# Differential attention: the squares of heads 0 to 6 computed on GpSimd, with two halving additions before VectorE's sum

## Chip, cores and metric

One Trainium2 chip, one of its cores. The metric is device microseconds from the first to the last instruction of the program. The kernel before takes 2082.36 us, the median of three runs (2082.19 to 2086.64).

## What is computed

The program runs two transformer stacks one after the other, each of two layers, over 256 tokens of width 1024. The first has gated feed-forward blocks, a short convolution and a sparse attention; the second has a differential attention and a grouped-query attention, each followed by a feed-forward block. The change lies in the differential attention alone. Of the reference, that part is:

```python
def attend(qb, keys, vals):
    s = jnp.einsum('bhmtd,bhmsd->bhmts', pair(qb), keys).astype(f32) * DIFF_DH ** -0.5
    p = jax.nn.softmax(s, axis=-1)
    a = (p[:, :, 0] - lam * p[:, :, 1]).astype(vals.dtype)
    return jnp.einsum('bhts,bhse->bhte', a, vals)

def finish(o):
    o = rmsnorm(o, subln) * (1.0 - lambda_init)
    return o.transpose(0, 2, 1, 3).reshape(Bt, Lt, DIFF_HEADS * 2 * DIFF_DH) @ w_out
```

There are 8 heads with outputs of 128 columns, and 512 queries: 256 latent tokens, which see 512 keys, and 256 context tokens, which see 256 keys. The `rmsnorm` in `finish` needs the sum of the squares of each head's 128 output columns, for every query. That sum is what the change computes in another way.

## The kernel before

The whole program is one `trace` function that writes five instruction streams by hand, one for each engine, with semaphore waits between them; no scheduler sets the order. Blocks are called sub-blocks s0 to s10, and the differential attention is s7. Queries lie in 4 tiles of 128 rows (the partitions), so that a head is 4 jobs: jobs 4h and 4h+1 are latent tiles with 512 keys ("full"), jobs 4h+2 and 4h+3 are context tiles with 256 keys ("half"). There are 32 jobs, J = 0 to 31.

Each job goes through these steps, and every engine has its own loop over J:

- TensorE computes the two score maps of the job into two PSUM banks (L2566), later transposes the combined probabilities (L2656), and later still multiplies them by the values (L2670). Its order for an index J is: scores of J, transposes of J-3, value product of J-4. The scores of J wait for the exponentials of J-2, since two bank pairs alternate; the transposes of J-3 wait for VectorE's step `p` of that job; the value product waits for ScalarE's copy of the transposes.
- VectorE takes the negated row maximum (L1898, `neg`), and for the job before, J-1, the reciprocal of a denominator (L1906), the coefficient (L1908, `coef`, 128x1, two inputs in SBUF) and the combination of the two maps (L1910, `p`, 128x512 or 128x256, two inputs in SBUF).
- ScalarE copies the transposes of J-3 out of PSUM (L1295, `evT`), then computes the two exponentials of J (L1270, `exp`).

When a head's four value products are done, ScalarE at index J = 4h+7 copies its output (128x512) from PSUM to SBUF (L1308, `evO`, the tile `ada`) and squares it into `silu_t[:, h % 2, :]` (L1312, `osq`). VectorE sums each group of 128 squares into one number, 4 per partition (L1890, `osum`), at its index J = 4h+8, behind step `p` of job 4h+7.

After the loop comes the tail. VectorE adds the epsilon term to the sums of heads 0 to 6 (L1920, `omean`), ScalarE takes the root (L1288, `root`, at its index 33, ahead of its copies of job 31 and of head 7's output), VectorE takes the reciprocal (L1925) and scales the heads (L1938, `on`); head 7 goes the same way a little later. TensorE transposes the scaled heads (L2685), ScalarE copies them (L1320), and the product with the output weights begins (L2305).

GpSimd does nothing in this sub-block. Its work elsewhere in the program is the low part of activations (L845, L853) and, in the sparse attention, a multiplication (L861).

Of the kernel before, what the change touches and what calls it, by code (L numbers as in the profile page):

```python
# [8 lines left out]
ALU = mybir.AluOpType  # L9
# [53 lines left out]
def trace(nc, t, io, out, stop):  # L63
    ctx = ExitStack()
    with ctx:
# [735 lines left out]
        def _(pool):  # L801
# [53 lines left out]
            def nsa_pool(tag):  # L855

                for J, (g_, tt, br, nk) in enumerate(nsa_jobs):
# [3 lines left out]
                    t.done(g.tensor_tensor(pr, pr, cf, ALU.mult), pool_s, (tag, "scaled", J))  # L861

            for s in subs:
                if s["T"] == 256:
                    for tt in range(2):
                        for k0, n in () if dve_lo(s) and tt else groups(s, tt):
                            lo(s, k0, n, tt)
                else:
                    for c in s["cs"][0:1] if second_pairs(s) and not pairs_late(s) else s["cs"]:
                        for k in s["ks"]:  # L870
                            lo_pair(s, k, c)
                if s["kind"] == "nsa":
                    nsa_pool(f"s{s['n']}")


        @block.scalar
        def _(act):
# [405 lines left out]
            def diff_act(s, tag, w):  # L1283
# [6 lines left out]
                for J in range(len(jobs) + 4):  # L1290
# [13 lines left out]
                    if 0 <= J - 4 and jobs[J - 4][1] == 3:  # L1304

                        h = jobs[J - 4][0]
                        act.wait_ge(pe_s, t.at((tag, "pv", J - 4)))
                        t.done(a.copy(w.qT[:, h, :], bank[6 + h % 2][:, :]), act_s, (tag, "evO", h))  # L1308
                        act.wait_ge(act_s, t.at((tag, "evO", h)))
                        if h >= 2:  # L1310
                            act.wait_ge(dve_s, t.at((tag, "osum", h - 2)))
                        t.done(a.activation(silu_t[:, h % 2, :], w.qT[:, h, :], ACT.Square), act_s, (tag, "osq", h))  # L1312
# [102 lines left out]
        def _(dve):  # L1415
# [470 lines left out]
            def diff_dve(s, tag, w):  # L1886
                jobs = diff_jobs
                def osum(h):
                    dve.wait_ge(act_s, t.at((tag, "osq", h)))
                    t.done(v.reduce_sum(ada_row[:, 4 * h:4 * h + 4], silu_t[:, h % 2, :].rearrange("p (t d) -> p t d", t=4), AX_X), dve_s, (tag, "osum", h))  # L1890
                for J in range(len(jobs) + 1):
# [9 lines left out]
                    if 0 <= J - 1:  # L1901
# [8 lines left out]
                        t.done(v.scalar_tensor_tensor(out=p0, in0=p1, scalar=d_coef(i), in1=p0, op0=ALU.mult, op1=ALU.add), dve_s, (tag, "p", i))  # L1910
                    if J >= 8 and J % 4 == 0:
                        osum((J - 8) // 4)
                gate(s, tag, 1)

                def means(a0, a1):
# [940 lines left out]
```

## Time and profile before

| | |
|---|---|
| median of three runs | 2082.36 us (2082.19 to 2086.64) |
| span of the profiled execution | 2082.3 us; the page gives no other time for it |
| TensorE, share of the span busy | 97% |
| VectorE | 66% |
| ScalarE | 45% |
| GpSimd | 4%, 121 instructions |
| mean granted TensorE clock | 0.991 |
| attention jobs of s7 in the trace | from about 1261.7 us to 1340 us |

The profiled execution's span agrees with the median to 0.1 us, so differences can be made against either. The shares are averages over eleven sub-blocks with different limits; for the change the stretch of s7 counts, and there each engine's own rows have to be read in order of time. VectorE's and ScalarE's durations are those of each instruction; consecutive instructions overlap by about 0.08 us, so the distance between two starts is shorter than the duration. Ends of TensorE's matmuls are modelled.

### The profile page before, as it was taken

The numbers are of one execution on the slowest core, as the hardware profiler recorded it, in microseconds if no ns is written. First come the engines' busy times: TensorE is split into PE (matmuls) and PEld (weight loads), VectorE is DVE, ScalarE is ACT, GpSimd is POOL, SyncE is SP. The second block draws the span as 40 slices with busy tenths as digits, with TensorE's granted clock in tenths as the row PEclk, the third lists the DMA queues.
The fourth block names the chain that finished last, engine by engine and source line by source line (L and its number), as shares of the span: only waits on it lengthen the run. The fifth ranks groups of instructions, "written<-read, shape, count | busy, mean of one in ns | idle before, by whom it ended". The sixth has DMA issues, their size and how long they took to land.

```text
span 2082.3 us, 32485 instructions
## 1 busy us (share of the span) xinstructions
PE 2024.0 (97%) x12969; PEld 1766.2 (85%) x12969; DVE 1377.4 (66%) x1936; ACT 940.4 (45%) x1420; POOL 88.9 (4%) x121
## 2 busy tenths in 40 slices
PE   6999999999999999999999999999999999999999
PEld 4998898998899987569988886688888888878997
DVE  3768798768976776657766756866555335855454
ACT  4344535334643445663355446842222323655342
POOL 1000000000100000310001000010000001100000
PEclk8999999999999999999999999999999999999999
DMA  9897877888877885647954321035344231425553
GB/s 348 277 316 281 297 260 263 302 271 313 273 257 268 303 292 188 226 148 264 303 180 152 113 90 41 12 111 174 130 139 164 81 112 61 142 81 198 180 177 113
DMA packets 240469, 411.32 MB, mean 198 GB/s; under 512 B 10236, under 2 KB 179669, under 8 KB 240341
## 3 DMA queue, kind: packets, MB, share of 16 engines
q1 hardware_dynamic: 239744, 409.31, 57.2%
q8 instruction: 89, 1.46, 0.3%
q14 instruction: 39, 0.32, 0.0%
q10 hardware_dynamic: 597, 0.23, 0.0%
HBM read 408.47 MB, written 1.05 MB: 197 GB/s over the span
## 4 chain that ended last, share of the span: by engine, by line
PE 79%; DVE 12%; ACT 4%; DMA 2%; issue 2%; SPq 0%; POOL 0%; DVEq 0%; ACTq 0%
PE bank L2305 21%; PE bank L2202 14%; PE bank L2204 13%; PE bank L2203 13%; DVE w_lo L1424 3%; PE bank L2395 2%; PE bank L2397 2%; PE bank L2396 2%; DVE gate_b L1480 2%; DMA xs<-in_ada_w 1%; DVE mid L1586 1%; PE bank L2154 1%; PE bank L2566 1%; ACT w_hi L890 1%; DVE astat L1898 1%
## 5 line engine op out<-in xcount | busy, mean ns | idle before, releaser
L1424 DVE TENSOR_TENSOR w_lo<-stage,w_hi 128x2048 fp32r<-128x2048 f32 x255 | 582.1, 2290 | 405.4 <-ACT w_hi L890 405.3
L890 ACT CAST w_hi<-stage 128x2048 fp32r<-128x2048 f32 x255 | 485.7, 1906 | 639.9 <-PE bank L2305 208.9
L2202 PE MATMUL bank<-h_hi,w_hi 128*128 128x256 f32 (+1 forms) x2336 | 699.3, 299 | 0.8 <-DVE w_lo L1424 0.8
L2203 PE MATMUL bank<-h_lo,w_hi 128*128 128x256 f32 (+1 forms) x2336 | 696.3, 298 | 0.0
L2204 PE MATMUL bank<-h_hi,w_lo 128*128 128x256 f32 (+1 forms) x2336 | 696.3, 298 | 0.0
L2202 PEld LDWEIGHTS bank<-h_hi,w_hi 128*128 128x128 f32 x2336 | 447.8, 192 | 14.3 <-DVE w_lo L1424 1.1
L2204 PEld LDWEIGHTS bank<-h_hi,w_lo 128*128 128x128 f32 x2336 | 447.7, 192 | 12.5
L2203 PEld LDWEIGHTS bank<-h_lo,w_hi 128*128 128x128 f32 x2336 | 447.8, 192 | 12.3
L2305 PE MATMUL bank<-w_hi,h_hi 128*128 128x512 f32 x776 | 244.0, 392 | 2.1 <-DVE mid L2066 1.2
L2305 PE MATMUL bank<-w_lo,h_hi 128*128 128x512 f32 x776 | 242.6, 390 | 0.0
L2305 PE MATMUL bank<-w_hi,h_lo 128*128 128x512 f32 x776 | 242.5, 390 | 0.0
L1480 DVE SCALAR_TENSOR_TENSOR gate_b<-ada,cond,gate_b 128x1024 f32<-128x1024 f32 x182 | 231.7, 1283 | 6.6 <-DMA ada<-in_kv_ada_w 1.2
L2305 PEld LDWEIGHTS bank<-w_hi,h_hi 128*128 128x128 f32 x776 | 144.3, 188 | 32.6 <-issue 1.7
L2305 PEld LDWEIGHTS bank<-w_hi,h_lo 128*128 128x128 f32 x776 | 145.8, 188 | 30.4
L2305 PEld LDWEIGHTS bank<-w_lo,h_hi 128*128 128x128 f32 x776 | 145.8, 188 | 30.4
L1367 ACT ACTIVATE silu_t<-bank 128x256 f32<-128x256 f32 (+1 forms) x132 | 53.7, 417 | 202.7 <-PE bank L2204 192.4
L1997 DVE TENSOR_TENSOR mid<-silu_t,bank 128x256 f32 (+3 forms) x132 | 60.1, 462 | 94.6 <-PE bank L2204 93.4
L1433 DVE TENSOR_TENSOR h_lo<-mid,h_hi 128x512 fp32r<-128x512 f32 (+1 forms) x82 | 64.3, 785 | 23.2 <-ACT h_hi L921 23.2
L2395 PE MATMUL bank<-w_hi,h_hi 128*128 128x512 f32 x192 | 75.9, 395 | 0.4 <-DVE w_lo L1424 0.4
L2397 PE MATMUL bank<-w_hi,h_lo 128*128 128x512 f32 x192 | 74.9, 390 | 0.0
L2396 PE MATMUL bank<-w_lo,h_hi 128*128 128x512 f32 x192 | 74.8, 390 | 0.0
L853 POOL TENSOR_TENSOR h_lo<-mid,h_hi 128x256 fp32r<-128x256 f32 x40 | 31.8, 822 | 831.4 <-ACT h_hi L994 831.4
(275 smaller groups left out, 2100.5 us busy)
## 6 DMA issues: line engine op xcount, KB each, us to landing
ada<-in_ada_w SPq DMA_DIRECT2D x114, 1024.0 KB, 5.5
stage<-in_ffn_w_in SPq DMA_DIRECT2D x88, 1024.0 KB, 9.1
stage<-in_ffn_w_out SPq DMA_DIRECT2D x44, 1024.0 KB, 5.1
stage<-in_ffn_w_gu SPq DMA_DIRECT2D x44, 1024.0 KB, 5.2
stage<-in_ffn_w_down SPq DMA_DIRECT2D x22, 1024.0 KB, 4.9
stage<-in_a_w_in SPq DMA_DIRECT2D x12, 1024.0 KB, 7.5
stage<-in_diff_w_in SPq DMA_DIRECT2D x12, 1024.0 KB, 5.4
ada<-in_kv_ada_w SPq DMA_DIRECT2D x8, 1024.0 KB, 7.4
```

What stands on the lines that cost most here:

```text
L890: a.copy(w_hi[:, s, :], stage[:, s, :]).then_inc(hi_done, 1)
L1424: v.tensor_tensor(w_lo[:, s, :], stage[:, s, :], w_hi[:, s, :].bitcast(F32), ALU.subtract).then_inc(lo_done, 1)
L1433: v.tensor_tensor(h_lo[:, r], mid[:, bass.ds(c, 2 * T)], h_hi[:, r].bitcast(F32), ALU.subtract).then_inc(mlo_done, 1)
L1480: ins = v.scalar_tensor_tensor(out=acc[c], in0=w, scalar=cond[:, b, kk, c:c + 1], in1=acc[c], op0=ALU.mult, op1=ALU.add)
L1997: v.tensor_tensor(mid[:, bass.ds(o, T)], silu_t[:, q, 0:T], bank[up_bank(s, j, i) + 2 + q][:, 0:T], ALU.mult).then_inc(mid_done, 1)
L2202: m.matmul(dst[:, 0:T], wh, h_hi[:, h0:h0 + T], start=(k == ks[0]), stop=False)
L2203: m.matmul(dst[:, 0:T], wh, h_lo[:, h0:h0 + T], start=False, stop=False)
L2204: ins = m.matmul(dst[:, 0:T], wl, h_hi[:, h0:h0 + T], start=False, stop=(k == ks[-1]))
L2305: ins = m.matmul(y_bank(T, tt, h)[:, :], a_[:, r:r + P], w_[:, slot, kc * D + h * 512:kc * D + (h + 1) * 512], start=first and n == 0, sto ...
L2395: m.matmul(bank[tt][:, :], h_hi[:, r], w_hi[:, slot, c], start=(k == 4), stop=False)
L2396: m.matmul(bank[tt][:, :], h_hi[:, r], w_lo[:, slot, c], start=False, stop=False)
L2397: ins = m.matmul(bank[tt][:, :], h_lo[:, r], w_hi[:, slot, c], start=False, stop=(k == 1))
```

## The change

For heads 0 to 6 ScalarE no longer squares. GpSimd waits for ScalarE's copy of the head, multiplies the head by itself (128x512), adds the upper 64 columns of each group of 128 to the lower 64 (4x64 numbers per partition), and the upper 32 of those to the lower 32 (4x32). Each of the three instructions waits for the one before it. VectorE then sums 32 numbers per group instead of 128. Head 7 is squared and summed as before. VectorE's sum of head h moves from index J = 4h+8 to J = 4h+10; the sum of head 6 then has no index in the loop and stands behind it.

```diff
+            def diff_pool(tag, w):
+
+                for J in range(len(diff_jobs) + 2):
+                    if J >= 9 and J % 4 == 1:
+                        h = (J - 9) // 4
+                        sq = silu_t[:, h % 2, :]
+                        pool.wait_ge(act_s, t.at((tag, "evO", h)))
+                        if h >= 2:
+                            pool.wait_ge(dve_s, t.at((tag, "osum", h - 2)))
+                        t.done(g.tensor_tensor(sq, w.qT[:, h, :], w.qT[:, h, :], ALU.mult), pool_s, (tag, "osq512", h))
+                        sq = sq.rearrange("p (t d) -> p t d", t=4)
+                        for n in (64, 32):
+                            pool.wait_ge(pool_s, t.at((tag, f"osq{8 * n}", h)))
+                            t.done(g.tensor_tensor(sq[:, :, 0:n], sq[:, :, 0:n], sq[:, :, n:2 * n], ALU.add), pool_s, (tag, "osq" if n == 32 else "osq256", h))
+
...
@@ -1306,9 +1323,10 @@
                         h = jobs[J - 4][0]
                         act.wait_ge(pe_s, t.at((tag, "pv", J - 4)))
                         t.done(a.copy(w.qT[:, h, :], bank[6 + h % 2][:, :]), act_s, (tag, "evO", h))
+                        if h < 7:
+                            continue
                         act.wait_ge(act_s, t.at((tag, "evO", h)))
-                        if h >= 2:
-                            act.wait_ge(dve_s, t.at((tag, "osum", h - 2)))
+                        act.wait_ge(dve_s, t.at((tag, "osum", h - 2)))
                         t.done(a.activation(silu_t[:, h % 2, :], w.qT[:, h, :], ACT.Square), act_s, (tag, "osq", h))
...
                 def osum(h):
-                    dve.wait_ge(act_s, t.at((tag, "osq", h)))
-                    t.done(v.reduce_sum(ada_row[:, 4 * h:4 * h + 4], silu_t[:, h % 2, :].rearrange("p (t d) -> p t d", t=4), AX_X), dve_s, (tag, "osum", h))
+                    n = P if h == 7 else P // 4
+                    dve.wait_ge(act_s if h == 7 else pool_s, t.at((tag, "osq", h)))
+                    t.done(v.reduce_sum(ada_row[:, 4 * h:4 * h + 4], silu_t[:, h % 2, :].rearrange("p (t d) -> p t d", t=4)[:, :, 0:n], AX_X), dve_s, (tag, "osum", h))
...
-                    if J >= 8 and J % 4 == 0:
-                        osum((J - 8) // 4)
+                    if J >= 10 and J % 4 == 2:
+                        osum((J - 10) // 4)
                 gate(s, tag, 1)
+                osum(6)
```

On VectorE, around head 0's sum, the order before is this. `gate_b` and `mid` hold the probabilities, `astat` the maxima and coefficients, `silu_t` the squares.

```order
L1910 SCALAR_TENSOR_TENSOR mid<-mid,astat 128x256
L1890 TENSOR_REDUCE ada_row<-silu_t 128x4
L1898 TENSOR_REDUCE astat<-bank 128x2
L1906 RECIPROCAL astat<-ada_row 128x1
L1908 SCALAR_TENSOR_TENSOR astat<-astat,stat,ada_row 128x1
L1910 SCALAR_TENSOR_TENSOR gate_b<-gate_b,astat 128x512
```

The same place of the changed kernel, where VectorE's lines are higher by 19:

```order
L1929 SCALAR_TENSOR_TENSOR mid<-mid,astat 128x256
L1917 TENSOR_REDUCE astat<-bank 128x2
L1925 RECIPROCAL astat<-ada_row 128x1
L1927 SCALAR_TENSOR_TENSOR astat<-astat,stat,ada_row 128x1
L1929 SCALAR_TENSOR_TENSOR gate_b<-gate_b,astat 128x512
L1917 TENSOR_REDUCE astat<-bank 128x2
L1925 RECIPROCAL astat<-ada_row 128x1
L1927 SCALAR_TENSOR_TENSOR astat<-astat,stat,ada_row 128x1
L1929 SCALAR_TENSOR_TENSOR gate_b<-gate_b,astat 128x512
L1909 TENSOR_REDUCE ada_row<-silu_t 128x4
L1917 TENSOR_REDUCE astat<-bank 128x2
```

The sum has moved behind two more jobs' steps, from in front of the maximum of a full job to in front of the maximum of a half job.

On GpSimd, which had nothing between the low parts of s7 and those of s8, this stands now for each of the heads 0 to 6:

```order
L853 TENSOR_TENSOR h_lo<-mid,h_hi 128x256 x16
L872 TENSOR_TENSOR silu_t<-ada 128x512
L876 TENSOR_TENSOR silu_t<-silu_t 128x4x64
L876 TENSOR_TENSOR silu_t<-silu_t 128x4x32
L872 TENSOR_TENSOR silu_t<-ada 128x512
```

In the tail, VectorE's last two jobs and head 6's sum stand in this order in the changed kernel; head 6's sum has kept its place:

```order
L1929 SCALAR_TENSOR_TENSOR mid<-mid,astat 128x256
L1925 RECIPROCAL astat<-ada_row 128x1
L1927 SCALAR_TENSOR_TENSOR astat<-astat,stat,ada_row 128x1
L1929 SCALAR_TENSOR_TENSOR mid<-mid,astat 128x256
L1909 TENSOR_REDUCE ada_row<-silu_t 128x4
L1937 TENSOR_TENSOR ada_row<-ada_row 128x28
L1940 SCALAR_TENSOR_TENSOR ada_row<-ada_row 128x28
```

## Rows read from the trace of the kernel before

**Rows 1.** Window of 10 us: busy us of PE, PEld, DVE, ACT, POOL; clock; DMA.

```profile
1295.00:1305.00 10.00, 9.75 (x64) 6.50 (x66) 9.51 (x23) 9.31 (x28) 0.00 (x0) 1.00 0.00 0
```

**Rows 2.** Chain of waits: start us, us, what. Part of one head.

```profile
1299.38 1.23 DVE astat L1898
...
1301.36 0.68 DVE ada_row L1890
```

**Rows 3.** Timeline of TensorE: start us, us. Scores of jobs 4, 8, 12.

```profile
1273.71 1.13 PE L2566 MATMUL bank<-mid,ada 64*128 64x512 f32 x4 [0.83 <-ACT mid L1270]
...
1281.85 1.13 PE L2566 MATMUL bank<-mid,ada 64*128 64x512 f32 x4
...
1290.02 1.13 PE L2566 MATMUL bank<-mid,ada 64*128 64x512 f32 x4
```

**Rows 4.** Timeline of VectorE, jobs 10 to 12 of the loop.

```profile
1298.79 0.48 DVE L1910 SCALAR_TENSOR_TENSOR mid<-mid,astat 128x256 f32<-128x256 f32 x1
1299.38 1.23 DVE L1898 TENSOR_REDUCE astat<-bank 128x2 f32<-128x1024 f32 x1
...
1300.70 0.22 DVE L1908 SCALAR_TENSOR_TENSOR astat<-astat,stat,ada_row 128x1 f32<-128x1 f32 x1
1300.96 0.48 DVE L1910 SCALAR_TENSOR_TENSOR mid<-mid,astat 128x256 f32<-128x256 f32 x1
1301.36 0.68 DVE L1890 TENSOR_REDUCE ada_row<-silu_t 128x4 f32<-128x512 f32 x1
1301.96 1.21 DVE L1898 TENSOR_REDUCE astat<-bank 128x2 f32<-128x1024 f32 x1
```

**Rows 5.** Timeline of ScalarE, the same stretch; idle time before it in brackets.

```profile
1299.37 0.58 ACT L1308 COPY ada<-bank 128x512 f32<-128x512 f32 x1
...
1303.21 0.69 ACT L1270 ACTIVATE gate_b<-bank,astat 128x512 f32<-128x512 f32 x1 [0.51 <-DVE astat L1898]
```

**Rows 6.** Groups by line of GpSimd, shapes apart: count | busy us, mean ns.

```profile
L845 POOL TENSOR_TENSOR h_lo<-mid,h_hi 128x512 fp32r<-128x512 f32 x14 | 18.8, 1359 | 863.4 <-ACT h_hi L978 863.4
L861 POOL TENSOR_TENSOR gate_b<-gate_b,w 128x512 f32<-128x512 f32 x8 | 8.3, 1040 | 44.4 <-DVE w L1794 44.4
...
L845 POOL TENSOR_TENSOR h_lo<-mid,h_hi 128x256 fp32r<-128x256 f32 x6 | 4.3, 740 | 0.4 <-ACT h_hi L978 0.4
...
L845 POOL TENSOR_TENSOR h_lo<-mid,h_hi 128x128 fp32r<-128x128 f32 x4 | 1.8, 461 | 19.1 <-ACT h_hi L978 19.1
```

**Rows 7.** Timeline of VectorE and GpSimd, sparse attention.

```profile
827.37 1.04 POOL L861 TENSOR_TENSOR gate_b<-gate_b,w 128x512 f32<-128x512 f32 x1 [37.49 <-DVE w L1794]
...
827.70 0.79 DVE L1773 TENSOR_TENSOR mid<-mid,w 128x60 f32<-128x60 f32 x1
...
842.10 0.22 DVE L1773 TENSOR_TENSOR mid<-mid,w 128x60 f32<-128x60 f32 x1
```

**Rows 8.** Timeline of VectorE and GpSimd, grouped-query attention.

```profile
1778.15 2.29 DVE L1424 TENSOR_TENSOR w_lo<-stage,w_hi 128x2048 fp32r<-128x2048 f32 x1
1779.14 3.27 POOL L853 TENSOR_TENSOR h_lo<-mid,h_hi 128x256 fp32r<-128x256 f32 x3 [13.89 <-ACT h_hi L994]
```

**Rows 9.** Timeline of GpSimd, start of the program: the second waits for the first.

```profile
5.30 0.40 POOL L825 CAST mid<-mid 128x256 f32<-128x256 int32 x1
5.84 0.40 POOL L827 TENSOR_SCALAR_AFFINE_SELECT mid<-mid 128x256 f32<-128x256 f32 x1
```

**Rows 10.** Timeline of VectorE, a sum over 128 numbers per partition.

```profile
1141.86 0.29 DVE L1816 TENSOR_REDUCE stat<-mid 128x2 f32<-128x128 f32 x1
```

**Rows 11.** Timelines of ScalarE and VectorE in the tail, in order of time.

```profile
1332.06 0.58 ACT L1308 COPY ada<-bank 128x512 f32<-128x512 f32 x1
...
1332.72 0.48 DVE L1910 SCALAR_TENSOR_TENSOR mid<-mid,astat 128x256 f32<-128x256 f32 x1
...
1334.23 0.19 DVE L1920 SCALAR_TENSOR_TENSOR ada_row<-ada_row 128x28 f32<-128x28 f32 x1
...
1335.45 0.23 ACT L1288 ACTIVATE ada_row<-ada_row 128x28 f32<-128x28 f32 x1
```

More of the change, by code:

```diff
@@ L873, in _ @@
                     nsa_pool(f"s{s['n']}")
+                elif s["kind"] == "diff":
+                    diff_pool(f"s{s['n']}", Wide(s))
         @block.scalar
```

## The prediction

> **What bounds the kernel now.** I read first the busy time of the stretch in which the change lies. Inside the loop over jobs TensorE is busy for 9.75 us of 10, VectorE for 9.51, ScalarE for 9.31 and GpSimd for none [rows 1]. Three engines are nearly full, so shares don't say which one sets the pace. The chain of waits is next: in each head it passes through VectorE's maximum and through its sum of squares [rows 2], 0.68 us that stand once in every head. By the chain alone one would expect a gain from a shorter sum. The timeline of TensorE answers that expectation. The scores of jobs 4, 8 and 12 start at 1273.71, 1281.85 and 1290.02 us [rows 3]. The distances are 8.14 and 8.17 us. The first distance holds no sum and no square at all, since head 0's output is copied only after it, and the second holds one of each. A whole square with a whole sum thus cost 0.03 us per head. TensorE's own work, and the order in which it takes the jobs, sets a period of about 8.14 us, and VectorE follows it with little to spare: its step `p` of job 10 starts at 1298.79, takes 0.48, of which about 0.08 overlap what follows, and the next maximum starts at 1299.38 [rows 4]. That is 0.19 us of idle time per head. ScalarE has 0.51 us of idle time in front of one exponential, where it waits for VectorE's maximum [rows 5].
>
> **The change, part by part, in one head.**
>
> ScalarE loses a square of 0.63 us. It was idle for 0.51 us of each head already and waits for VectorE there [rows 5], so I cost this gain at nothing in the loop. What hides it is ScalarE's wait for the maximum.
>
> VectorE loses a sum of 0.68 us, 0.60 from start to start (1301.36 to 1301.96) [rows 4]. It gains one over 4x32 numbers two jobs later. A sum over 128 numbers took 0.29 us [rows 10], so 0.21 after the same overlap. The relief is 0.39 us per head. It can be cashed only down to TensorE's 8.14, so at most 0.03 per head.
>
> GpSimd gets three instructions. The nearest rows for the square are 1.36 us (a subtraction, 128x512) and 1.04 us (a multiplication of the same size in which one operand repeats); the additions are 0.74 and 0.46 us by their sizes [rows 6]. I take 1.31 for the square, near the upper row, since both of its operands run through all numbers, and 0.72 and 0.44 for the additions, a little under the means, which contain disturbed cases. The Trainium skill's page "GPSIMD Engine Reference", section Performance versus the Vector engine, gives 4497 ns for an addition of 2048 numbers; a quarter of it, an estimate of 1.12 us, would make the square's hold below shorter by 0.2 us in each head. The three take 2.47 us and two hand-overs. A hand-over from one GpSimd instruction to the next that waits for it was 0.14 us (5.30 + 0.40 to 5.84) [rows 9]. From the end of ScalarE's copy, 1299.95 [rows 5], the squares are ready at about 1302.8. The short sum stands two jobs behind the old place at 1301.36 [rows 4], and a job is a quarter of 8.17 us, so it is due at about 1305.4; nobody waits for GpSimd in the loop. It was idle there, so its own work is free.
>
> What isn't free is the memory access. Two rows of the sparse attention show it: VectorE's L1773, 128x60 with two inputs in SBUF, takes 0.22 us, but 0.79 when it starts at 827.70, inside a GpSimd multiplication that ends at 828.41, and it ends 0.08 us after that end [rows 7]. The other way round, three GpSimd instructions of 0.74 [rows 6] took 3.27 us, 1.05 too many, where the first began 1.3 us before the end of a VectorE instruction with two SBUF inputs (1778.15 + 2.29) [rows 8]. The later one stands still until the earlier one is through. The Trainium skill's page "SBUF — State Buffer", section Who interferes with whom, states the rule, which speaks against this change: a VectorE instruction with two SBUF inputs and a GpSimd instruction that reads SBUF exclude each other for the whole of whichever came first, while a `tensor_reduce` is never held. The trace agrees for the two pairs shown. Had the two engines been free of each other, the sum would be that of the third rival below.
>
> Now the place. The copy of a head ends at 1299.95, so the square runs from about 1300.03 to 1301.34. `coef` of job 11, two SBUF inputs, is due at 1300.70 [rows 4]. It ends about 1301.42 instead of 1300.92: 0.50 us late (0.25 with the lower price of the square). Then `p` of job 11 and GpSimd's first addition are both due within 0.1 us of each other. `p` needs `coef`'s end and about 0.04 (1300.92 to 1300.96 [rows 4]), so it is due at 1301.46; the addition is due at 1301.34 and a hand-over of 0.14, at 1301.48. I take it that `p` wins. Then the addition waits, is over about 1302.5, and the second one about 1303.1, beside a maximum that reads PSUM and isn't held. VectorE's account for the head is 0.50 - 0.60 + 0.21 = +0.11 us, less than its 0.19 of slack. Against that the delay comes in one lump, between a maximum and the transposes that wait for `p`, so I don't cost it at nothing: 0.10 us per head, with 0 and 0.2 as ends. For the six heads inside the loop this is **+0.6 us**.
>
> **The tail.** Head 6's copy ends at 1332.64 [rows 11]. GpSimd starts at about 1332.72, in the same moment as the last `p` [rows 11]; without a hold it is done after 2.47 and two hand-overs of 0.14, at 1335.5. The short sum, 0.29, ends at 1335.85 and the epsilon step, 0.19 [rows 11], at 1336.1. ScalarE's root, which waited for its table and started at 1335.45 [rows 11], starts then. That is 0.65 later. Behind the root on ScalarE's queue stand the copy of job 31's transposes, the gate's copies, head 7's copy and its square, and TensorE's last value product waits for the first of these; I take it that nothing in that queue has time to spare. ScalarE's missing square doesn't help, as it would only wait longer at the root. So the tail costs **+0.6 us**, with +0.1 (square of 1.04, short hand-overs) and +1.2 (the square held by the last `p`) as ends.
>
> After s7 the down product follows on TensorE, which is the bound again, and hands the delay on. Nothing moves on SP's queue; no DMA is touched.
>
> The sum is 0.6 + 0.6 = 1.2 us on 2082.3, and the median is the same to 0.1: **2083.6 us**. A measurement of this kernel can tell about 0.2%, 4.2 us, from no change.
>
> **The rivals.**
>
> The first ends slower. GpSimd's addition gets in front of `p` in each head. It decides by 0.02 us in my account above: with a hand-over under 0.12 us, the addition goes first. Then the addition runs from 1301.44 to 1302.16, and `p` of job 11 ends at about 1302.50 (the last 0.34 of its 0.48 are left, by the overlap that L1773 showed) instead of 1301.94: another 0.56 us. The account is 1.06 - 0.60 + 0.21 = +0.67; less the 0.19 of slack, and with the same 0.10 for the lump, it is 0.58 per head, 3.5 for six, and with 0.7 for the tail 2086.5. With the square at 1.04 it is 2084.9; if the last addition also catches a `coef`, 0.44 less slack, near 2088.5. For it: the order is nearly a tie, and VectorE's 9.51 of 10. Against it: the measured 0.14.
>
> The second is that the relief counts in full. VectorE is on the chain of waits [rows 2], and 0.39 us in seven heads is 2.7 us: 2079.6. Against it stands the first head with no sum and the same period [rows 3].
>
> The third is that the change does nothing that can be seen: `coef` is so small that it isn't held, or GpSimd's square falls beside the maximum only. Then the loop gains 0.03 x 6 = 0.2 and the tail takes 0.2 to 0.6: 2082.5.
>
> **How the numbers follow.** My forecast has 0.44, the slow rival 0.27, the neutral one 0.21, the gain 0.08. Of the slow rival a little over half lies above 2086.5, which makes 0.15 for slower by over 0.2%. A gain of over 4.2 us would need more than the whole relief, so I leave 0.03, for what I haven't seen. The rest, 0.82, is within 0.2%. The range leaves out the gain below and the upper part of the slow rival: 2081.6 to 2087.2.
>
> **What would show it.** In the profile after, the distance of every fourth score should be 8.2 to 8.3 us from head 2 on; about 8.7 would be the slow rival, 8.14 the neutral one. L1927 should have a longest instance near 0.7 us in each head, beside many of 0.22, and L1929 should stay at 0.75 and 0.48; a L1929 above 1 us in each head is the slow rival. GpSimd's addition of 4x64 should be longer than 0.74 where `p` holds it. The root should start about 1.2 us later. I am wrong if GpSimd's square takes over 1.6 us, if the summed squares come so late that VectorE waits for them, or if the period falls under 8.1.

## The result, and the profile after

The changed kernel takes 2093.96 us, the median of five runs (2089.05 to 2096.19). The kernel before takes 2085.93 (2082.19 to 2087.99), the median of five too, of which three are the runs that I started from. The ratio is 1.0036, with an interval of 1.0026 to 1.0047: 7.5 us slower by the ratio, 8.0 between the medians, and outside my range of 2081.6 to 2087.2. The profiled execution of the changed kernel took 2089.05 us, with a span of 2087.3 at a mean granted clock of 0.990.

Lines from 1890 on are higher by 19 or 20 now: the maximum is L1917, `coef` L1927, `p` L1929, VectorE's sum L1909. GpSimd's square is L872, its additions L876. The same window as [rows 1], and the next one; the columns are those of [rows 1]:

```profile
1295.00:1305.00 10.00, 9.56 (x65) 6.35 (x63) 9.65 (x21) 8.63 (x26) 3.38 (x5) 1.00 0.01 2
1305.00:1315.00 10.00, 9.56 (x66) 6.42 (x62) 9.72 (x19) 8.19 (x25) 3.47 (x5) 1.00 0.00 0
```

VectorE lost 0.40 us of work per head and is yet busier than before (9.65 and 9.72 against 9.51), while TensorE is down from 9.75 to 9.56. Something has made VectorE's instructions longer. The timeline of VectorE in the same place as [rows 4], the last half job of head 2 and what follows, shows which:

```profile
1302.98 1.22 DVE L1917 TENSOR_REDUCE astat<-bank 128x2 f32<-128x1024 f32 x1
1304.12 0.15 DVE L1925 RECIPROCAL astat<-ada_row 128x1 f32<-128x1 f32 x1
1304.31 0.57 DVE L1927 SCALAR_TENSOR_TENSOR astat<-astat,stat,ada_row 128x1 f32<-128x1 f32 x1
1304.92 1.03 DVE L1929 SCALAR_TENSOR_TENSOR mid<-mid,astat 128x256 f32<-128x256 f32 x1
1305.88 1.21 DVE L1917 TENSOR_REDUCE astat<-bank 128x2 f32<-128x1024 f32 x1
```

And the timeline of GpSimd beside it:

```profile
1303.83 1.04 POOL L872 TENSOR_TENSOR silu_t<-ada 128x512 f32<-128x512 f32 x1 [6.05 <-ACT ada L1325]
1304.95 1.32 POOL L876 TENSOR_TENSOR silu_t<-silu_t 128x256 f32<-128x256 f32 x2
```

`coef` takes 0.57 instead of 0.22. It is held until about the end of the square: 1303.83 + 1.04 = 1304.87, and `coef` ends at 1304.88. Then `p` takes 1.03 instead of 0.48. The first addition runs inside it, from 1304.95 for about 0.74 us, and `p` ends at 1305.95, some 0.26 us behind that addition's end. The addition itself is not lengthened. So in heads 1 to 5 both instructions are held, 0.35 and 0.55 us, and it is `p` that stands still, not the addition. In head 0 `coef` is held for 0.15 only (it takes 0.37), which is why the second distance below is shorter than the later ones; in head 6 `p` alone is held, for 0.84. The groups of GpSimd, shapes apart, show the durations over all seven heads:

```profile
L872 POOL TENSOR_TENSOR silu_t<-ada 128x512 f32<-128x512 f32 x7 | 7.3, 1039 | 175.5 <-ACT ada L1325 175.5
L876 POOL TENSOR_TENSOR silu_t<-silu_t 128x256 f32<-128x256 f32 x7 | 5.2, 736 | 0.5
L876 POOL TENSOR_TENSOR silu_t<-silu_t 128x128 f32<-128x128 f32 x7 | 3.5, 507 | 0.5
```

The square costs 1.04 us, the lower of my two prices. TensorE now waits, here as in the heads around it, for an exponential that waited for VectorE's late maximum. The first row is TensorE's, the scores of a half job; the second ScalarE's, the exponential before it:

```profile
1308.63 0.70 PE L2586 MATMUL bank<-mid,ada 64*128 64x256 f32 x4 [0.44 <-ACT gate_b L1287]
```

```profile
1307.12 0.69 ACT L1287 ACTIVATE gate_b<-bank,astat 128x512 f32<-128x512 f32 x1 [0.87 <-DVE astat L1917]
```

ScalarE's wait was 0.51 us there before [rows 5].

**A local measure.** All executions of this program spread over some 10 us, so I read each profile in the stretch that the change can touch: from the scores of job 4 (the first of [rows 3]) to the start of the product with the output weights (the expectations below call it the down product), and in it the distances of every fourth score. Read from TensorE's timeline of each profile, in us:

| kernel | scores of job 4 start | distances of jobs 4, 8, ... 28 | stretch |
|---|---|---|---|
| before | 1273.71 | 8.14 8.17 8.18 8.17 8.18 8.17 | 70.31 |
| after | 1276.88 | 8.14 8.30 8.49 8.48 8.49 8.49 | 72.44 |
| e1_same_before | 1277.67 | 8.14 8.18 8.18 8.17 8.17 8.18 | 70.32 |
| e2_same_after | 1281.23 | 8.14 8.29 8.50 8.48 8.49 8.49 | 72.43 |
| e3_add_after_p | 1279.37 | 8.15 8.14 8.15 8.14 8.14 8.15 | 70.86 |
| e4_no_sums | 1279.42 | 8.14 8.14 8.15 8.15 8.14 8.15 | 70.14 |
| e5_square_only | 1275.90 | 8.14 8.14 8.33 8.34 8.33 8.33 | 71.06 |
| e6_writes_only | 1275.79 | 8.14 8.14 8.15 8.14 8.14 8.14 | 69.78 |
| e7_square_after_p | 1275.19 | 8.14 8.15 8.27 8.43 8.43 8.42 | 72.81 |
| e8_same_after | 1282.40 | 8.15 8.29 8.48 8.48 8.49 8.48 | 72.41 |
| e9_extra_sum | 1275.05 | 8.14 8.76 8.76 8.76 8.76 8.77 | 73.84 |
| e10_three_heads | 1280.40 | 8.15 8.29 8.48 8.49 8.15 8.16 | 71.61 |
| e11_same_after | 1272.13 | 8.14 8.30 8.49 8.48 8.49 8.50 | 72.43 |
| e12_wider_add | 1278.78 | 8.13 8.58 8.75 8.76 8.75 8.76 | 74.33 |

The same kernel repeats its stretch within 0.03 us, where the whole time varies by several us. Two single executions, of 3116.69 us in e1 and of 5746.66 us in e2, lie far outside this spread and are left out of all ratios. In the stretch the change costs 2.1 us: 1.9 up to the start of the last `p` (59.01 us from the scores of job 4 before, 60.90 after) and 0.2 behind it. The measured 7.5 us are more than that; what lies in the rest is taken up with e8 and e11.

### The profile page after: what moved, and what is told of

Same layout as the page of the kernel before. It is cut to its first block, busy times and chain, and to the rows that moved or that the text cites. A ratio compares the mean times of both kernels' runs of the same rounds, so it can differ in the third digit from the quotient of the medians.

```text
span 2087.3 us, 32499 instructions
## 1 busy us (share of the span) xinstructions
PE 2026.0 (97%) x12969; PEld 1767.2 (85%) x12969; DVE 1380.2 (66%) x1936; ACT 937.6 (45%) x1413; POOL 104.9 (5%) x142
## 4 chain that ended last, share of the span: by engine, by line
PE 81%; DVE 10%; ACT 4%; issue 2%; DMA 2%; SPq 0%; POOL 0%; DVEq 0%; ACTq 0%
PE bank L2325 20%; PE bank L2222 14%; PE bank L2224 14%; PE bank L2223 14%; DVE w_lo L1442 2%; PE bank L2415 2%; PE bank L2417 2%; PE bank L2416 2%; DVE gate_b L1498 1%; PE bank L2586 1%; DVE mid L1604 1%; DMA xs<-in_ada_w 1%; PE bank L2174 1%; ACT w_hi L907 1%; PE bank L2564 1%
## 5 line engine op out<-in xcount | busy, mean ns | idle before, releaser
L845 POOL TENSOR_TENSOR h_lo<-mid,h_hi 128x512 fp32r<-128x512 f32 (+2 forms) x24 | 24.9, 1059 | 882.1 <-ACT h_hi L995 882.1
```

## The experiments

The kernels were timed in three batches: e1 to e4, e5 to e8, e9 to e12. The kernels of one batch share the runs of the kernel before; each has 12 runs of its own. Ratios are to the kernel before of the same batch. Diffs are against the changed kernel where nothing else is said.

### e1_same_before and e2_same_after: how well the two kernels repeat

Both kernels again, unchanged.

> The kernel before, unchanged, measured against itself. It shows how far two sets of runs of one kernel lie apart, and with which granted clocks. Between the profiles of before and after, job 4's scores start 3.2 us later (1273.71 against 1276.88), ahead of anything the change touches; from there to the first down product it is 70.3 us before and 72.4 after, so only 2.1 us belong to the changed stretch. Theory A (the change costs about 2 us, the rest of the 8 us between the medians is the clock's chance): this kernel's own runs spread by 5 to 8 us too, with clocks between 0.986 and 0.991, and the time follows the clock. Theory B (the change costs 7 to 8 us by itself, by some effect outside its stretch): this kernel's runs stay near 2082 to 2086 with a clock near 0.991, and only the changed kernel goes to 2090 and more.

> The changed kernel, unchanged, once more. Theory A: the ratio to the kernel before is 1.001, within 0.2% of 1, when clocks are alike, and the stretch from job 4's scores to the down product is again 72.4 us in the profile. Theory B: the ratio is again 1.003 to 1.004 and the clock is again lower than that of the kernel before.

The kernel before gave 0.9995 [0.9982, 1.0008], the changed one 1.0018 [1.0006, 1.0030]. The stretches came out at 70.32 and 72.43, as in the first profiles. The sign is sure; the size of the first comparison, 1.0036, is not repeated.

### e3_add_after_p: the first addition waits for `p`

```diff
                             pool.wait_ge(pool_s, t.at((tag, f"osq{8 * n}", h)))
+                            if n == 64:
+                                pool.wait_ge(dve_s, t.at((tag, "p", 4 * h + 7)))
```

> One wait more: GpSimd's first addition of head h also waits for VectorE's step p of job 4h+7, so that the addition can't get in front of it. The slow rival says that the addition's hold of p (1.04 us where 0.48 is normal) makes the period 8.49 us instead of 8.17. If so, p takes 0.48 again in this kernel, only coef stays held (0.57), the period of every fourth score goes back to 8.14 to 8.2, and the stretch from job 4's scores to the down product is 70.3 to 71 us. If instead the held coef or GpSimd's square makes the period, it stays near 8.4 to 8.5 and the stretch above 72.

The ratio is 0.9997 [0.9984, 1.0009], and the stretch is 70.86 instead of 72.44. The timeline of VectorE, the same place (its lines are higher by two, and the whole is 2.0 us later):

```profile
1306.31 0.57 DVE L1929 SCALAR_TENSOR_TENSOR astat<-astat,stat,ada_row 128x1 f32<-128x1 f32 x1
1306.92 0.48 DVE L1931 SCALAR_TENSOR_TENSOR mid<-mid,astat 128x256 f32<-128x256 f32 x1
1307.52 1.23 DVE L1919 TENSOR_REDUCE astat<-bank 128x2 f32<-128x1024 f32 x1
```

and of GpSimd:

```profile
1305.83 1.04 POOL L872 TENSOR_TENSOR silu_t<-ada 128x512 f32<-128x512 f32 x1 [5.17 <-ACT ada L1327]
1307.55 1.26 POOL L878 TENSOR_TENSOR silu_t<-silu_t 128x256 f32<-128x256 f32 x2 [0.68 <-DVE mid L1931]
```

`coef` is still held by 0.35 (0.16 in head 0), `p` is back at 0.48, and every distance is back at 8.14 to 8.15. So the hold of `p` is what the loop pays for, and the hold of `coef` alone fits under TensorE's period. This is the order that my forecast assumed. With it the loop is even 0.03 us per head faster than before; the 0.10 us per head that I had put on the lump of delay does not exist. What is left, +0.55 us, is all in the tail.

### e4_no_sums: the relief by itself, at its largest

Against the kernel before: ScalarE doesn't square heads 0 to 5, VectorE doesn't sum them, and their sums are the constant 1.

```diff
                         t.done(a.copy(w.qT[:, h, :], bank[6 + h % 2][:, :]), act_s, (tag, "evO", h))
+                        if h < 6:
+                            continue
...
-                    if J >= 8 and J % 4 == 0:
-                        osum((J - 8) // 4)
+                    if J == 32:
+                        osum(6)
```

> From the kernel before: heads 0 to 5 are neither squared nor summed on any engine (their sums are the constant 1), heads 6 and 7 as before. If TensorE's work sets the period, it is 8.14 us instead of 8.17 and the stretch from job 4's scores to the down product falls by 0.2 us from 70.3. If VectorE's sum on the chain of waits is worth its time, the stretch falls by 6 x 0.60 = 3.6 us and the period to about 7.6.

The ratio is 0.9999 [0.9986, 1.0012]; the stretch is 70.14, so six squares and six sums, 7.9 us of work on two engines, are worth 0.17 us in all. The distances are TensorE's 8.14. The time went into waiting. VectorE's timeline has this in front of the maximum of job 4h+8:

```profile
1307.57 1.23 DVE L1899 TENSOR_REDUCE astat<-bank 128x2 f32<-128x1024 f32 x1 [0.47 <-PE bank L2567]
```

The `p` before it starts at 1306.62 and takes 0.48, and the next instruction can follow 0.08 before an end, so 1307.57 - 1307.02 = 0.55 us are free in this place. VectorE's sum of 0.60 used to fill them and stood out by 0.05, which is the 0.03 that the distances show.

### e5_square_only: the square on GpSimd, no additions

GpSimd squares, and VectorE sums all 128 numbers per group, two jobs later as in the changed kernel.

```diff
-                        t.done(g.tensor_tensor(sq, w.qT[:, h, :], w.qT[:, h, :], ALU.mult), pool_s, (tag, "osq512", h))
...
+                        t.done(g.tensor_tensor(sq, w.qT[:, h, :], w.qT[:, h, :], ALU.mult), pool_s, (tag, "osq", h))
...
-                    n = P if h == 7 else P // 4
+                    n = P
```

> From the changed kernel: GpSimd's two additions are gone, VectorE sums all 128 numbers of each group at the new place. With no addition nothing can hold p, but coef is still held by the square (0.57 instead of 0.22). Theory (VectorE's account against TensorE's period, holds counted): per head +0.35 for coef, the sum costs 0.60 as before, slack 0.19, so the period is 8.3 to 8.45 us and p takes 0.48 everywhere but at head 6. If only the hold of p matters and a late coef is free, the period is 8.14 to 8.18, since VectorE's work is then that of the kernel before.

The ratio is 1.0002 [0.9988, 1.0016], with a stretch of 71.06. `coef` is held (0.58), `p` is not, except in the last head. The distances of 8.33 are 0.19 above TensorE's, although only 0.36 are held: here the whole sum of 0.60 stands two jobs later. What is free behind that place are the 0.19 us in front of the next head's maximum of 4h+7 and what the hold leaves of the 0.55 in front of that of 4h+8, 0.19 too. That leaves 0.22 over.

### e6_writes_only: GpSimd as busy, but reading nothing

The square and the additions are replaced by writes of the constant 1, so the sums are those of ones.

```diff
-                        t.done(g.tensor_tensor(sq, w.qT[:, h, :], w.qT[:, h, :], ALU.mult), pool_s, (tag, "osq512", h))
+                        t.done(g.memset(sq, 1.0), pool_s, (tag, "osq512", h))
...
-                            t.done(g.tensor_tensor(sq[:, :, 0:n], sq[:, :, 0:n], sq[:, :, n:2 * n], ALU.add), pool_s, (tag, "osq" if n == 32 else "osq256", h))
+                            t.done(g.memset(silu_t[:, h % 2, :], 1.0), pool_s, (tag, "osq" if n == 32 else "osq256", h))
```

> From the changed kernel: each of GpSimd's three instructions is a memset of 128x512 numbers in silu_t, about 0.5 us each, at the same place and with the same waits. GpSimd is then busy for about 1.5 us beside coef and p, but reads nothing. If the hold is one of reading (two inputs of VectorE against GpSimd's reads), coef takes 0.22 and p 0.48 throughout, and the period is 8.14 us. If any GpSimd instruction holds VectorE's, coef or p is longer in every head and the period is above 8.2.

The ratio is 0.9991 [0.9976, 1.0006], with a stretch of 69.78. The groups of VectorE, shapes apart:

```profile
L1929 DVE SCALAR_TENSOR_TENSOR mid<-mid,astat 128x256 f32<-128x256 f32 x14 | 6.8, 484 | 0.5
L1927 DVE SCALAR_TENSOR_TENSOR astat<-astat,stat,ada_row 128x1 f32<-128x1 f32 x28 | 6.1, 220 | 1.0
```

Nothing is held, though each of GpSimd's three writes takes 0.52 us, they begin in the same place, and in each of heads 1 to 5 the second begins inside `coef` and lasts into `p`. So writing SBUF doesn't hold VectorE; what the held cases have beside it is GpSimd's reading. The Trainium skill's page "SBUF — State Buffer", section Who interferes with whom, names the same pair, a VectorE instruction with two SBUF inputs and a GpSimd instruction that reads SBUF, "not with one that only writes it"; the trace agrees on both halves, with 0.57 against 0.22.

### e7_square_after_p: the square itself waits for `p`

```diff
+                        pool.wait_ge(dve_s, t.at((tag, "p", 4 * h + 7)))
                         t.done(g.tensor_tensor(sq, w.qT[:, h, :], w.qT[:, h, :], ALU.mult), pool_s, (tag, "osq512", h))
```

> From the changed kernel: GpSimd's square of head h waits for VectorE's step p of job 4h+7, so that all three of GpSimd's instructions come later by one step. The same work, the same order on VectorE. If the place of GpSimd's instructions against VectorE's decides, the first addition now meets coef of the full job 4h+8 and the second meets its p, and the period is 8.3 to 8.5 us although job 4h+7 is never held. If a late start frees VectorE, as the wait in the third experiment did (8.15), the period is 8.14 to 8.2.

The ratio is 1.0011 [0.9997, 1.0025], with a stretch of 72.81: locally no better than the change. VectorE's timeline, one job further on:

```profile
1304.80 0.60 DVE L1928 SCALAR_TENSOR_TENSOR astat<-astat,stat,ada_row 128x1 f32<-128x1 f32 x1
1305.43 1.04 DVE L1930 SCALAR_TENSOR_TENSOR gate_b<-gate_b,astat 128x512 f32<-128x512 f32 x1
```

and of GpSimd:

```profile
1303.54 1.04 POOL L873 TENSOR_TENSOR silu_t<-ada 128x512 f32<-128x512 f32 x1 [6.05 <-DVE mid L1930]
1304.66 1.26 POOL L877 TENSOR_TENSOR silu_t<-silu_t 128x256 f32<-128x256 f32 x2
```

The square now lies beside the maximum, which it doesn't hold, but the two additions behind it outlast the maximum. From head 2 on they catch `coef` and the longer `p` of the next job, 0.38 and 0.29 us. Waiting for the right instruction is not enough: what is released by it must also be through before VectorE's next pair of reads. e3 has only the additions there, and they are, by 0.04 us: in the place shown above the second ends at 1308.81, and the next `coef` starts at 1308.85.

### e8_same_after and e11_same_after: the changed kernel again

Unchanged, beside the kernels of the second and of the third batch.

> The changed kernel once more, on the chip and in the hour of the three above, for the ratio alone: 1.0036 and 1.0018 were measured so far, 1.0010 is what its own stretch (72.4 against 70.3 us) accounts for. If the remainder is chance of the clock, this ratio may fall anywhere from 0.999 to 1.003; if it belongs to the kernel, it is again 1.0015 or more.

> The changed kernel a fourth time, beside the two above, for the ratio: 1.0036, 1.0018 and 1.0022 so far. If the excess over the 1.0010 of its own stretch is the kernel's, it is again above 1.0015; if it was chance, between 0.9995 and 1.0025.

The ratios are 1.0022 [1.0008, 1.0035] and 1.0017 [1.0004, 1.0030], with stretches of 72.41 and 72.43. These and e2 ask what lies outside the stretch. The changed kernel reached the scores of job 4 at 1276.88, 1281.23, 1282.40 and 1272.13 us in its four profiles, the kernel before at 1273.71 and 1277.67. The code up to there is the same in both, and the earliest of all is a run of the changed kernel. So no profile shows a delay that belongs to the change and lies ahead of it. None shows one behind the stretch either: from the start of the product with the output weights to the end it takes 737.97, 738.24, 737.90 and 740.31 us in the changed kernel's four profiles, 738.27 and 738.02 in those of the kernel before. The 740.31 are e11's, whose clock was 0.97 from 1800 to 1850 us, where that of the kernel before was 1.00. What moves ahead of the stretch is the granted clock. Windows of the stretch with the sparse attention, for the kernel before, for the changed kernel, and for e11:

```profile
750.00:1000.00 250.00, 240.36 (x1657) 189.56 (x1656) 170.50 (x449) 132.11 (x295) 31.01 (x28) 0.97 0.65 222
```

```profile
750.00:1000.00 250.00, 239.43 (x1627) 188.12 (x1626) 168.35 (x447) 128.77 (x291) 31.00 (x28) 0.95 0.63 216
```

```profile
750.00:1000.00 250.00, 240.38 (x1664) 189.73 (x1663) 170.38 (x448) 131.72 (x293) 31.03 (x28) 0.97 0.65 222
```

The changed kernel of the first profile ran at 0.95 there, e11 at 0.97 like the kernel before. Over the 252 executions with a listed clock (without the two left out above), a fit with one offset per kernel and one slope gives 1.5 us more for each 0.001 of mean clock less, and the single executions lie between about 0.984 and 0.992. The 40 of the changed kernel have a mean of 2092.3 us at 0.9878, 116 of the kernel before 2087.4 at 0.9888. Of these 4.9 us the stretch has 2.1, the clock about 1.4, and 1.4 (with an uncertainty of about 0.7) I can't place. My expectations don't decide whether this is chance: the repetitions came out at 1.0017 to 1.0022, above the 1.0015 that I had set for an excess of the kernel's own, but in e8 and e11 also inside the range that I had given to chance. The stretch alone accounts for 1.0010. Why the mean clock of the changed kernel's runs was lower, in each of the three batches, stays open too.

### e9_extra_sum: VectorE made later in the same place, without GpSimd

Against the kernel before, an extra sum over 96 numbers per group in front of the real one, heads 0 to 5.

```diff
                     dve.wait_ge(act_s, t.at((tag, "osq", h)))
+                    if h < 6:
+                        t.done(v.reduce_sum(ada_row[:, 4 * h:4 * h + 4], silu_t[:, h % 2, :].rearrange("p (t d) -> p t d", t=4)[:, :, 0:96], AX_X), dve_s, (tag, "extra", h))
+                        dve.wait_ge(dve_s, t.at((tag, "extra", h)))
```

> From the kernel before: for heads 0 to 5 VectorE sums 4x96 of the squares once more in front of each head's sum, about 0.5 us from start to start, and GpSimd does nothing. It slows VectorE as much as the holds do, by other means. Theory (a period of 8.14 by TensorE and 0.19 us of slack on VectorE): the period is 8.4 to 8.55 us and the stretch from job 4's scores to the down product 71.8 to 72.5. As to the 3 us by which the changed kernel's runs lie above its own stretch: if they come with any slower loop, this kernel's runs also lie some 4 to 5 us above the kernel before; if they need GpSimd, only by about 2 us.

The ratio is 1.0017 [1.0004, 1.0030], with a stretch of 73.84, 3.5 us more. I had expected at most 72.5, and a distance of at most 8.55. VectorE's timeline:

```profile
1303.47 0.49 DVE L1913 SCALAR_TENSOR_TENSOR mid<-mid,astat 128x256 f32<-128x256 f32 x1
1303.88 0.55 DVE L1891 TENSOR_REDUCE ada_row<-silu_t 128x4 f32<-128x384 f32 x1
1304.46 0.69 DVE L1893 TENSOR_REDUCE ada_row<-silu_t 128x4 f32<-128x512 f32 x1
```

The extra sum delays the maximum by 0.58 us and the distance grows by 0.59, from 8.17 to 8.76. In front of this maximum the kernel before had nothing left to absorb. The 0.19 us of idle time that I had counted as slack stand elsewhere, in front of the maximum before it (1299.38 in [rows 4]), and are still there in e9. The delay needs no GpSimd: time that VectorE loses here is lost whatever takes it. The measured time agrees with the stretch, 3.5 us by both. It shows no excess like the changed kernel's, though its interval, 0.8 to 6.3 us, is too wide to exclude one of 1.4.

### e10_three_heads: half a dose

GpSimd squares heads 0 to 2 alone; ScalarE squares the others and VectorE sums them whole, at the new place.

```diff
-                    if J >= 9 and J % 4 == 1:
+                    if J >= 9 and J % 4 == 1 and J < 21:
...
-                        if h < 7:
+                        if h < 3:
```

> From the changed kernel: only heads 0 to 2 go through GpSimd, heads 3 to 7 are squared by ScalarE and summed by VectorE in full, at the new places. The period should be 8.3 to 8.5 where heads 1 and 2 are held and 8.17 from then on, and the tail as in the kernel before, since GpSimd isn't in it: the stretch is 70.31 plus about 0.6 = 70.9 to 71.1 us. If the additions' hold isn't what costs, the period stays 8.4 or more to the end.

The ratio is 1.0011 [0.9998, 1.0024], with a stretch of 71.61, where I had expected at most 71.1. Three distances are those of the changed kernel (8.29, 8.48, 8.49), and with the next one the loop is back at 8.15, with a whole sum two jobs later. The holds leave no trace behind them; each head pays for itself. The stretch is 1.3 us longer, of which the distances have 0.71. The other 0.59 lie behind job 28, where nothing of GpSimd runs: from the scores of job 28 to the last `p` it takes 10.59 us (1330.12 to 1340.71) against 10.00 before. That is the size of head 5's whole sum, 0.60. My reading, which no run tests by itself, is that at the new place it has no later head whose free time takes it up, so the moved sum is paid for once, at the end.

### e12_wider_add: the first addition made longer

The first addition takes 96 numbers per group instead of 64, so the sums are others.

```diff
-                            t.done(g.tensor_tensor(sq[:, :, 0:n], sq[:, :, 0:n], sq[:, :, n:2 * n], ALU.add), pool_s, (tag, "osq" if n == 32 else "osq256", h))
+                            m_ = 96 if n == 64 else 32
+                            t.done(g.tensor_tensor(sq[:, :, 0:m_], sq[:, :, 0:m_], sq[:, :, P - m_:P], ALU.add), pool_s, (tag, "osq" if n == 32 else "osq256", h))
```

> From the changed kernel: GpSimd's first addition is over 4x96 numbers instead of 4x64 (the sums are then others). By GpSimd's own rows (0.74 us for 256, 0.46 for 128) it takes 1.02 instead of 0.74. If p stands still for the whole addition, p of job 4h+7 takes 1.3 us instead of 1.04 and the period is 8.49 + 0.28 = 8.77 us, the stretch 74 us or a little more. If the hold is a fixed price per meeting, p stays at 1.04 and the period at 8.49.

The ratio is 1.0023 [1.0009, 1.0038], with a stretch of 74.33. GpSimd's group of the addition, and VectorE's held `p`:

```profile
L877 POOL TENSOR_TENSOR silu_t<-silu_t 128x384 f32<-128x384 f32 x7 | 7.0, 1006 | 0.5
```

```profile
1306.75 0.57 DVE L1928 SCALAR_TENSOR_TENSOR astat<-astat,stat,ada_row 128x1 f32<-128x1 f32 x1
1307.36 1.31 DVE L1930 SCALAR_TENSOR_TENSOR mid<-mid,astat 128x256 f32<-128x256 f32 x1
```

The addition is 0.27 us longer (1.006 against 0.736), `p` 0.28 (1.31 against 1.03), the distance 0.27 (8.76 against 8.49). `coef` is unchanged. The length of the first addition goes one to one into `p` and from there into the period. Together with e3 this settles the mechanism in the loop.

### One account for all of them

This account was made after the runs, and the two free times in it are read from e4. The distance is 8.14, TensorE's own, plus what VectorE does or loses in front of two maxima beyond what is free there: 0.19 us in front of that of job 4h+7 and 0.55 in front of that of job 4h+8 (e4). A sum at the new place, in front of job 4h+10, comes ahead of both of the next head. A hold or a sum between the two finds only the second (e9):

| kernel | in front of job 4h+8 | at the new place | account | measured distance |
|---|---|---|---|---|
| before | sum 0.60 | nothing | 8.14 + 0.05 | 8.17 |
| after | holds 0.35 + 0.55 | 0.20 | 8.14 + 0.36 | 8.49 |
| e3 | hold 0.35 | 0.20 | 8.14 | 8.14 |
| e5 | hold 0.36 | 0.60 | 8.14 + 0.22 | 8.33 |
| e9 | sums 0.58 + 0.60 | nothing | 8.14 + 0.63 | 8.76 |
| e12 | holds 0.35 + 0.83 | 0.20 | 8.14 + 0.64 | 8.75 |

The held instructions of e7 stand behind the maximum of job 4h+8, and the account doesn't cover them.

No kernel here beats the one before by more than 0.53 us in the stretch, and those that come nearest (e4, e6) leave out the squares. TensorE's 8.14 us is the floor, so I tried no better placement.

## Why the prediction was wrong

**That TensorE sets the period and the relief can't be cashed: right.** I gave it at most 0.03 us per head. e4 takes away more work than the change does and gains 0.17 us in six heads. The rival with the full relief falls.

**That GpSimd's reads hold `coef`: right, a little mis-sized.** I had 0.50 with a square of 1.31, and 0.25 with one of 1.04. The square took 1.04, so the lower row of [rows 6] was the better one, a multiplication in which not all operands run through different numbers. The hold was 0.35, more than the 0.25 for this price, because the square starts 0.48 us before `coef` (1303.83 to 1304.31) and not 0.67 as in my account. The estimate of 1.12 us from the Trainium skill's page "GPSIMD Engine Reference", section Performance versus the Vector engine, was nearer than the row that I took. Where `p` isn't held and the short sum is kept, this term costs nothing in the loop, as e3 shows; with the whole sum (e5) it costs a part of the 0.19 per head there.

**"I take it that `p` wins": this step failed.** It decided the forecast. I let `p` win by being due 0.02 us earlier. Two terms of that were off, and they nearly cancel: the hand-over between GpSimd instructions is 0.08 (1303.83 + 1.04 to 1304.95) and not 0.14 [rows 9], and `coef` ends 0.01 us behind the square and not 0.08. So the recorded starts have the order of the forecast, `p` 0.03 us ahead (1304.92 against 1304.95), and `p` is held all the same, in each of heads 0 to 5. What failed is the assumption that at such a distance the one that is due first gets through. I had named a hand-over under 0.12 as the sign of the rival, and it came; that it is what decides the order, no run shows. `p` then lost 0.55 us, where the rival had 0.56. e3 turns this one order round and takes 1.6 us of the 2.1 away; e12 lengthens the winner and moves the loop one to one.

**The price of the slow rival: nearly double in the loop.** I had 0.58 per head. The account with the measured numbers is 0.90 held, less 0.60, plus 0.20, less 0.19 of slack: 0.31, and the distances rose by 0.31 to 0.32. The difference is the square of 1.31 and the lump of 0.10. The lump was a guess; e3, where `coef` is late by 0.35 and the distance stays at 8.14, shows none of it. That the account closes with the 0.19 is partly luck: the moved sum of 0.20 takes up just these, while the holds meet the other 0.55, which the old sum used to fill. e9 shows that the 0.19 don't help a delay in front of job 4h+8.

**The tail: right in sign, smaller.** From the last `p` to the root it took 1337.78 to 1340.96, 3.18 us, against 2.73 before [rows 11], so the root is 0.45 later and not 0.65. From the root to the output product it took 8.36 instead of 8.57, so 0.21 of this were made up again and the tail costs 0.24, not 0.6. The last `p` too is held, and longer than any other: it starts in the same moment as the square.

```profile
1337.78 1.32 DVE L1929 SCALAR_TENSOR_TENSOR mid<-mid,astat 128x256 f32<-128x256 f32 x1
1340.25 0.29 DVE L1909 TENSOR_REDUCE ada_row<-silu_t 128x4 f32<-128x128 f32 x1 [1.15 <-POOL silu_t L876]
1340.74 0.19 DVE L1940 SCALAR_TENSOR_TENSOR ada_row<-ada_row 128x28 f32<-128x28 f32 x1
```

```profile
1340.96 0.23 ACT L1305 ACTIVATE ada_row<-ada_row 128x28 f32<-128x28 f32 x1 [1.00 <-DVE ada_row L1940]
```

VectorE's short sum waits 1.15 us for GpSimd, as forecast, and the root waits for the epsilon step. I had said that ScalarE's missing square doesn't help in the tail. That was wrong: the load of the root's table stands behind it, so the table comes earlier. It starts 1.08 us behind the start of the last `p` before (first line) and 0.42 behind it now (second line):

```profile
1333.80 1.28 ACT L1090 ACT_TABLE_LOAD   x1
```

```profile
1338.20 1.28 ACT L1107 ACT_TABLE_LOAD   x1
```

In the kernel before the root started as soon as its queue was through; now its queue was ready 1.00 us before it. In e6, where the constants are ready early, the stretch behind job 28 is 20.93 us against 21.30 before.

**The sum.** The slow rival's local cost would have been 4.2 us by my prices; it is 2.1. Added to the 2082.3 of the profile before, that is 2084.4, inside my range, but the median was 2093.96. The range was built on differences in one profile, and it left out two things. The first is that the span of a profile is not the time of its execution: wherever both are listed, the time is 1.7 or 1.8 us above the span. By this the profiled execution of the kernel before took about 2084.0 us, and that its span agreed with the median of 2082.36 was luck. The second is that executions of this program differ by several us with the granted clock: the profile before was at 0.991, the five runs of the changed kernel had a mean of 0.9874. At 1.5 us for each 0.001 this is 5.3 us. Even the kernel before came out at 2085.93 when two more runs were added to the three that I started from, 3.6 above their median. The mean of the changed kernel's five runs is 2093.4 us, 9.4 above 2084.0. Of these, 2.1 us are shown to be the change; 5.3 are the clock's, by the fit and not by an experiment; and 2.0 are open, as 1.4 are over all repetitions. So the failed step explains most of the 2.1 us in the stretch, 1.6 of them, but it is not what put the time outside the range.

## What to carry to other kernels

An engine that looks free isn't, where its reads shut out a neighbour: before work goes to GpSimd, lay its instructions beside VectorE's two-input instructions in order of time, and see which of them falls beside a maximum, which reads PSUM and isn't held. A tie of some hundredths of a microsecond between two engines should be forecast as undecided, whichever side the sum of the starts favours, and its worse side priced, or settled by one wait in the program as in e3. And slack belongs to a place: idle time in front of one instruction doesn't pay for a delay in front of the next.

## What was unexpected

**Who wins a near tie.** In each of heads 0 to 5 the record of `p` starts 0.02 or 0.03 us before that of the addition, as here in head 1, first VectorE's row, then GpSimd's:

```profile
1296.43 1.04 DVE L1929 SCALAR_TENSOR_TENSOR mid<-mid,astat 128x256 f32<-128x256 f32 x1
```

```profile
1296.46 1.33 POOL L876 TENSOR_TENSOR silu_t<-silu_t 128x256 f32<-128x256 f32 x2
```

Yet `p` is the one held. By the recorded starts VectorE was first. Whether its first read comes later than its recorded start, or an instruction that was already waiting is preferred, no run here separates. The hold is inside the recorded duration of the held instruction, so it shows as a longer instruction and not as idle time: VectorE's busy time rises while it does less.

**The speed of GpSimd.** One size, 128x512, took 1.36 us for a subtraction of two tiles [rows 6] and 1.04 for a square, whose two operands are the same numbers. The additions of two different ranges were 0.74 and 0.51 us for 256 and 128 numbers; the shorter one takes 0.46 in e3 and e7, so 0.05 of the 0.51 stand only where it starts beside the rest of the held `p`. So the square costs 2.0 ns per number, the subtraction of the same size 2.7, and the longer addition 2.9. Whether the repeated operand or the operation makes the difference, no run here separates.
